# Queries of the expert stage: the first column group as two of 256, copies of x one order step later, a tile's end bank by bank

## The reference

```python
def block(hb):                                      # 128 tokens
    q = (hb @ w_query).reshape(128, 8, 2, 128)      # w_query: 2048 x 2048
    s = einsum('thpc,hpnc->thpn', q, sub_keys)      # two scores per head, 128 keys each
    top_s, top_i = lax.top_k(s, 16)
    cand_s = top_s[:, :, 0, :, None] + top_s[:, :, 1, None, :]
    cand_i = top_i[:, :, 0, :, None] * 128 + top_i[:, :, 1, None, :]
    best_s, best_j = lax.top_k(cand_s, 16)
    idx = take_along_axis(cand_i, best_j)           # 16 of 16384 experts
    g = softmax(best_s)
    a = gelu(einsum('thkd,td->thk', u[idx], hb))
    return einsum('thk,thkd->td', g * a, v[idx])    # added to x
```

## Time and profile before

| | |
|---|---|
| Runs, median (lowest, highest) | 3162.84 us (3162.42, 3167.22), three runs |
| The profiled execution's own time | 3161.82 us |
| Its span, from first to last instruction | 3159.6 us |
| Busy in the span | PE 69%, DVE 54%, ACT 27%, POOL 26% |
| Moved by DMA | 901 MB, 285 GB/s over the span |

### The profile page before, as it was taken

How to read it: one execution, slowest core, us unless ns; L and a number is a source line. 1 busy time by engine, 2 the same in 40 slices (tenths; PEclk the granted TensorE clock), 3 DMA queues, 4 the chain that set the end, 5 groups by cost and what they waited for, 6 DMA issues and landing times.

```text
span 3159.6 us, 30717 instructions
## 1 busy us (share of the span) xinstructions
PE 2164.9 (69%) x12338; PEld 1487.2 (47%) x12338; DVE 1692.1 (54%) x2583; ACT 853.3 (27%) x1267; POOL 806.4 (26%) x680
## 2 busy tenths in 40 slices
PE   5899999989999999999989973223222222322335
PEld 2666677877778787667668872000000000000001
DVE  3436556654756664343335688665565555565430
ACT  1333443443444454454545421000000000000000
POOL 1111100000000000000000026665555555555552
PEclk8999999999999999999989987665666666666667
DMA  9888865557665555343325689999999999999998
GB/s 385 285 294 271 287 213 153 181 166 243 207 190 157 152 178 158 116 134 106 107 86 162 207 323 406 422 422 421 422 421 422 421 422 420 422 421 422 421 422 338
DMA packets 243593, 901.00 MB, mean 285 GB/s; under 512 B 20374, under 2 KB 45228, under 8 KB 177004
## 3 DMA queue, kind: packets, MB, share of 16 engines
q0 software_dynamic: 94208, 612.85, 48.3%
q1 hardware_dynamic: 148768, 285.58, 27.9%
q10 hardware_dynamic: 476, 0.62, 0.1%
HBM read 894.78 MB, written 2.10 MB: 284 GB/s over the span
## 4 chain that ended last, share of the span: by engine, by line
PE 56%; DMA 30%; DVE 7%; ACT 3%; issue 2%; POOL 2%; SPq 0%; DVEq 0%; ACTq 0%; POOLq 0%
PE pp L1786 48%; DMA late<-in_peer_v,MI 9%; PE tp L1786 6%; DMA P<-in_peer_v,MI 5%; DMA x<-in_peer_v,MI 5%; DMA ring<-in_peer_v,MI 4%; DMA SY<-in_peer_v,MI 2%; DVE wL L1112 2%; PE tp L1789 2%; DMA late<-in_w_mod 2%; ACT wH L613 1%; DMA ring<-in_peer_w_query 1%; POOL late L2319 1%; DMA ring<-in_w_in 1%; DMA P<-in_w_mod 0%
## 5 line engine op out<-in xcount | busy, mean ns | idle before, releaser
L1112 DVE TENSOR_TENSOR wL<-ring,wH 128x1024 fp32r<-128x1024 f32 (+3 forms) x504 | 583.8, 1162 | 765.0 <-ACT wH L613 763.7
L1786 PE MATMUL pp<-wH,hH 128*128 128x512 f32 (+3 forms) x1888 | 747.8, 396 | 16.2 <-issue 7.9
L613 ACT ACTIVATE wH<-ring 128x1024 fp32r<-128x1024 f32 (+3 forms) x504 | 508.0, 1010 | 784.8 <-PE pp L1786 650.8
L1786 PE MATMUL pp<-wH,hL 128*128 128x512 f32 (+3 forms) x1888 | 718.3, 380 | 0.0
L1786 PE MATMUL pp<-wL,hH 128*128 128x512 f32 (+3 forms) x1888 | 717.7, 380 | 0.0
L1786 PE MATMUL pp<-late,S 128*32 128x512 f32 x768 | 234.5, 892 | 336.9 <-DMA x<-in_peer_v,MI 157.9
L1786 PEld LDWEIGHTS pp<-wH,hH 128*128 128x128 f32 x1888 | 360.0, 191 | 159.5 <-issue 90.6
L1786 PEld LDWEIGHTS pp<-wH,hL 128*128 128x128 f32 x1888 | 359.2, 190 | 63.6
L1786 PEld LDWEIGHTS pp<-wL,hH 128*128 128x128 f32 x1888 | 360.8, 191 | 56.1 <-issue 1.0
L1745 DVE CUSTOM_DVE_ANT_0 late<-late,P 128x2048 f32<-128x2048 f32 x84 | 191.3, 2288 | 154.0 <-DMA late<-in_peer_u,MI 153.8
L1786 PE MATMUL pp<-P,S 128*32 128x512 f32 x360 | 157.8, 873 | 166.8 <-DMA late<-in_peer_v,MI 91.4
(11 more groups left out here) (303 smaller groups left out, 2925.5 us busy)
## 6 DMA issues: line engine op xcount, KB each, us to landing
ring<-in_w_in SPq DMA_DIRECT2D x288, 512.0 KB, 4.0
ring<-in_w_out SPq DMA_DIRECT2D x96, 512.0 KB, 4.4
P<-in_w_mod POOLq DMA_DIRECT2D x85, 512.0 KB, 4.9
late<-in_w_mod SPq DMA_DIRECT2D x64, 512.0 KB, 9.4
SY<-in_w_mod POOLq DMA_DIRECT2D x43, 512.0 KB, 5.1
ring<-in_w_in SPq DMA_DIRECT2D x48, 368.0 KB, 4.6
ring<-in_peer_w_query SPq DMA_DIRECT2D x32, 512.0 KB, 7.2
ring<-in_w_in SPq DMA_DIRECT2D x24, 344.0 KB, 3.2
```

What stands on the lines that cost most here:

```text
L613: act(heads(wH[k % NB][:, 0:2 * wd], 2), raw, ACT.Copy).then_inc(*tick("act_hi", ("hi", k)))
L1112: tt(lo, raw, hi.bitcast(F32), ALU.subtract).then_inc(*tick("dve_lo", *names))
L1786: return e.matmul(o, l, r, start=start, stop=stop, skip_group_check=skip)
```

## The change

- `G_QUERY` makes the first group of `w_query` two groups of 256 columns, head 0 and head 1. There are now five groups and 40 pieces: 16 of 256 KB and 24 of 512 KB.
- The scores and the choice of head 0 are placed behind piece 8, those of head 1 behind piece 16. `FIRST_DOT` is 13, so that 27 dots stand between the pieces where there were 20.
- `hidden 0` and `hidden 1` move to pieces 8 and 10 (from 6 and 4). `nf` moves from `U` to `S`, since the scores of head 0 may now be written before hidden rows are read.
- The copies of x become a step of their own, `turn_x`, placed at piece 6, and `late_loads` moves into the projection before.
- At a tile's end each bank has its own mark `summed`, and is added as soon as it is complete. The stores are by bank, 32 rows x 512 columns of 64 KB each: 16 for a tile, 8 on SP's queue and 8 on ACT's.

```diff
-GROUPS = [G_IN, G_OUT, G_IN, G_OUT, G_IN2, G_OUT, G_OUT]
+G_QUERY = cgroups((0, 2, 256), (512, 3, 512))
+GROUPS = [G_IN, G_OUT, G_IN, G_OUT, G_IN2, G_OUT, G_QUERY]
...
-FIRST_DOT = 12
+FIRST_DOT = 13
...
         if n == 1:
             yield "sub_keys",
+            yield "late_loads",
...
-    yield "late_loads",
     for q, (g, c0, w, pc) in enumerate(PIECES[6]):
         yield from splits(6, q)
         if q == 3:
             yield "norm", 6
+        if q == 6:
+            yield "turn_x",
         if q == 2:
             yield "chunk", 6, 3
             yield "skip_pair",
-        if q in (4, 6):
-            yield "hidden", (6 - q) // 2
+        if q in (8, 10):
+            yield "hidden", q // 2 - 4
         yield "piece6", q
-        if g == 1 and pc == 0:
-            yield "scores", 0
+        if q in (8, 16):
+            yield "scores", 0, q // 16
             yield "skip_pair",
+        if q == 8:
             yield "open", "X", "choose", 0
-        if g == 1:
-            yield from pump(4, 0, 0)
-        if q == FIRST_DOT - 1:
+        if q in (8, 9):
+            yield from pump(3, 0, 0)
+        if 16 <= q < 23:
+            yield from pump(1, 0, 0)
+        if q == 23:
             yield "drain", "X"
         if q >= FIRST_DOT:
             yield "dot", 0, q - FIRST_DOT
...
-        nf = U[:, 0:2048]
+        nf = S[:, 0:2048]
...
-                if n == 34 - FIRST_DOT:
+                if n == len(PIECES[6]) + 2 - FIRST_DOT:
                     queue = list(range(5, NG)) + queue
...
+            def store_rows(t, parts, sem):
+                for d in range(4):
+                    w.wait_ge(*at("added", t, d))
+                    for q in parts:
+                        e.dma_start(rows_d[t, 32 * q:32 * q + 32, d * 512:(d + 1) * 512],
+                                    xP[q:128:4, t, d * 512:(d + 1) * 512]).then_inc(*landed(sem, ("out", t, d, q)))
...
-                    w.wait_ge(*at("added", t, 3))
-                    for q in range(4):
-                        e.dma_start(rows_d[t, 32 * q:32 * q + 32, :], P[q:128:4, 0, t * D:(t + 1) * D]).then_inc(
-                            *landed("out_done", ("out", t, q)))
+                    store_rows(t, (0, 1), "out_done")
...
-                    w.wait_ge(*at("mixed", 4 * t + 3, 7))
                     for d in range(4):
+                        w.wait_ge(*at("summed", t, d))
                         v = xP[:, t, d * 512:(d + 1) * 512]
                         tt(v, v, pp[d][:, :], ALU.add).then_inc(*tick("dve_h", ("added", t, d)))
...
+                elif what == "turn_x":
                     w.wait_ge(*at("x added", 5, 3, 1))
                     for t in range(2):
                         for q in range(4):
```

More of the change, by code:

```diff
@@ L345, in order @@
         if i < 7:
-            yield "scores", i + 1
+            yield "scores", i + 1, None
             yield "open", "X", "choose", i + 1
-        for j in range(0 if i else 32 - FIRST_DOT, 32):
+        for j in range(0 if i else len(PIECES[6]) - FIRST_DOT, 32):
             yield "dot", i, j
@@ L1066, in scalar @@
                     w.wait_ge(*at("turned", u))
-                    w.wait_ge(*(at("chosen", i - 2) if i > 1 else at("hidden", 0)))
-                    act(sc[i % 2], tp[u % 2][:, 0:512], ACT.Copy, scale=rsd[:, 4 + i // 4:5 + i // 4]).then_inc(*tick("act_h", ("pair free", u), ("scores", i)))
+                    if i > 1:
+                        w.wait_ge(*at("chosen", i - 2))
+                    w.wait_ge(*at("rstd", 6))
+                    h0, h1 = (0, 2) if a[1] is None else (a[1], a[1] + 1)
+                    act(sc[i % 2][:, 256 * h0:256 * h1], tp[u % 2][:, 0:256 * (h1 - h0)], ACT.Copy,
+                        scale=rsd[:, 4 + i // 4:5 + i // 4]).then_inc(
+                        *tick("act_h", ("pair free", u), *[("scores", i, h) for h in range(h0, h1)]))
+                elif what == "add":
+                    store_rows(a[0], (2, 3), "out_act_done")
                 elif what == "gelu":
@@ L2249, in tensor @@
                     w.wait_ge(*at("chunk", 6, pc // 2))
-                    for b in range(4):
+                    for b in range(wd // 128):
                         for k2 in range(2):
```

32 lines of the change are left out of this document (22 added, 10 removed).

## The result

| | kernel before | changed kernel |
|---|---|---|
| Median of 12 runs | 3164.22 us (3155.29 to 3171.22) | 3169.41 us (3161.94 to 3173.62) |
| Ratio, 95% interval | | 1.0019 [1.0011, 1.0027] |
| Span of the profiled execution | 3159.6 us | 3160.0 us |

The changed kernel is slower by 0.19%, some 6 us, and the interval lies clear of no change. The prediction had 3165.5 within 3156 to 3172, and 0.65 for a change under 0.2%; 3169.4 lies just above the 3169.2 that it named as that bound, the ratio just under it.

The account below looks back on a forecast made before the run. The prediction took DMA to bound the expert stage. Its terms, -5.1 + 10.4 + 0 - 2.5 = +2.8 us, gave 3164.6 for the profiled execution and 3165.5 for the median, range 3156 to 3172.

Parts of the forecast that it names:

- second rival: Expert stage, pieces 16 to 23: DVE becomes the bound with head 1's choice there; 7 us idle DMA, 3172.5, chance 0.17.
- first gather: Start of the expert stage: head 0 projected sooner, so the first gather comes 5.1 us earlier, bounds 13 and 3.4.
- left to move behind it: Loads behind the first gather: 24 of 512 KB instead of 16, 4.19 MB more, costing 10.4 us at 401 GB/s.
- gaps behind the first gather: Mixed stretch of gathers and loads: no added DMA idle time, 0 us, bounds -2.7 and +5.
- end of a tile: Last adds and stores: three of four adds fall under the matmuls, saving 2.5 us, bounds 1.9 and 3.2.
- The copies of x: Query projection: copies issued where they stood, starving loads beside them; PE idles 5.9 us ahead of piece 6, then half clock.
- The rival that rested on it: Query projection: loads don't starve beside the copies, first gather 13 us earlier, total 3157.7, chance 0.17.
- DVE stays behind cover: From head 0's numbers to the last cut: DVE needs 96.7 us, DMA 107, so DVE adds no time.
- The sign of the last paragraph: Mixed stretch: the forecast is wrong if the DMA share falls under 0.95.
- The other sign: Start of the expert stage: the forecast is wrong if the first gather comes before 1825.
- The gaps close: Third rival: 2.7 us lost behind the first gather and 2.6 around the last cut vanish; 3160.3, chance 0.06.
- The second choice of POOL's: Unit 1's choice, after the last cut: POOL's 6.96 us wait grows by up to 2 under queued transfers, costing 0.

Follow-up runs that it names:

- e4: Changed kernel with head 1's choice in one block behind piece 16 instead of a step behind each of pieces 16 to 22; ratio 1.0019 to the kernel before.
- e6: Changed kernel without head 1's choice for unit 0, its expert numbers copied from head 0; ratio 1.0011 to the kernel before.
- e2: Changed kernel with the copies of x made to wait for the cut of piece 6; ratio 1.0003 to the kernel before.
- e3: Changed kernel with the copies of x made to wait for the cut of piece 10; ratio 1.0005 to the kernel before.
- e5: Changed kernel with the 16 loads of pieces 24 to 39 bringing only 128 of their 256 rows; ratio 1.0004 to the kernel before.
- e7: Changed kernel with copies of x behind the cut of piece 6 and both hidden instructions behind head 0's numbers; ratio 1.0004 to the kernel before.
- e1: Kernel before with only the new end of a tile put in; ratio 0.9993 to the kernel before.
- e8: Changed kernel with copies and hidden instructions later, cuts between head 0's choice steps, head 1's choice ahead of the first dot; ratio 1.0002 to the kernel before.
- e9: As e8, but each of the eight copies of x waits for a cut of its own, pieces 6 to 13; ratio 0.9988 to the kernel before.

## Why the prediction was right or wrong

**The range held, one term of the sum didn't, and part of the hit is luck.** The forecast's sum was +2.8 us; the pair of profiles has +7.2 and the runs some +6. By its own mechanism the forecast spanned 3161 to 3169, which 3169.4 just misses; the range held it because it reached nearly to the second rival's price. In the sum a first gather that came earlier than forecast hid a third of the term that failed. The terms, as the prediction put them, and as measured:

| Term | forecast | measured |
|---|---|---|
| first gather | -5.1 (-13 to -3.4) | -7.4 |
| left to move behind it | +10.4 | +10.0 |
| gaps behind the first gather | 0 (-2.7 to +5) | +6.8 |
| end of a tile | -2.5 (-3.2 to -1.9) | -2.3 |
| sum | +2.8 | +7.2 |

**The copies of x:** right. They were issued 1.2 us behind the first query matmul (before 1.3), and a load beside them took 12.0 us. PE stood 4.3 us instead of 5.9, in two pauses instead of one (in e4 and e6, the same up to there, in one of 4.3), and head 0 was projected at 18.7 us instead of 20.8 behind the first query matmul: the 1.6 us less of idle time are most of that. The half clock came as forecast: 0.50 over the 12 matmuls of piece 6, which took 2.9 us, and full pace again in piece 7. From there to the first gather it was 16.1 us, 16.3 forecast. The rule of the Trainium skill that queues take turns packet by packet ("DMA: Bandwidth & Descriptors", Queues, rings and completion order) was read as giving the loads a fair part. It speaks of packets, and says that such a packet holds some 9 to 17 descriptors; whether the profile's packets are these, no run here shows. Counted in the profile's packets one stretch looks like it (97 to 112, with 5.5 KB against 1 KB still only 15% of the time); the stretches with 63 to 27, 89 to 226, and 59 to none don't agree. The rival that rested on it failed, but its first gather, 13 us earlier, is what e2 and e3 have (42.2 - 29.3 = 12.9), once the copies wait.

**The bytes:** right, 24 loads and 4.22 MB. e5 adds what the term hid: such bytes are worth their transfer time only while DMA decides. Taking as many out again was worth 5.7 us.

**The gaps: the step that failed.** "DVE stays behind cover" came from a sum over the whole stretch, 96.7 us of DVE work in 107 us of DMA work. The sum was good (from head 0's numbers to the last cut, 112 us, DVE worked 94.8); the mean was the wrong question. A piece with a step of the choice needs up to 5.7 us of DVE where DMA needs 3.74, the others have only a tenth to spare, and what is in flight (five sets) didn't carry the difference beyond 1863. The prediction had this as its second rival, at 0.17, with a price of 7 us; e6 measured 6.9, for some 10 us less of DVE work (11.7 in e4's block, of which e6 keeps 1.5), and e7 showed that other DVE work behind the first gather is charged too. The sign of the last paragraph came: a share of 0.93 from 1870 to 1900, under its 0.95, and 0.82 from 1863 to 1886. So did the condition that the rival named: DVE waited for the starved loads of four cuts (0.8 to 2.2 us each, the last until 1858.8), and from then on every set had landed before its dot began. The other sign, a first gather before 1825, came only in time from the span's start (1821.0): counted from the first query matmul, its bound is 32.0 and the gather came at 34.8. The rival should have had the better part of the chance, since its working (4.8 us of DVE for a piece against 3.9 of DMA) needed no guess, and the one thing against it, the absorbing by what is in flight, was only asserted. With that rival's 3172.5 and the 2.3 us by which the first gather was forecast too late, the time would have come out at 3170.2; the median was 3169.4.

**The gaps close** (the third rival): mostly not. The first 10 us behind the first gather lost 3.6 us (3.0 before), the 9.8 us at the last cut 1.5 (2.6 before, in 11.5).

**The second choice of POOL's** (unit 1): forecast to wait up to 2 us longer than the 6.96 of the earlier trace rows, and to cost nothing. It waited 7.29:

```profile
1972.20 0.94 POOL L2349 DMA_INDIRECT late<-in_peer_u,MI  x1 [7.29 <-DVE MI L1691]
```

**The end:** right, mechanism and size (the profiles of after and e1; the ratio of e1 alone doesn't tell it from nothing).

## What to carry to other kernels

When one resource decides and a second runs at 90% of it, a forecast has to be made piece by piece and not for the stretch: work that a change puts on the second, in the time when it refills the first, is charged for the most part (here 6.9 us for some 10, and 3.8 for 2.35). In the kernel before the same choice stood under the first five gathers, and 6.9 us less were lost; but e8, which put it back there with more beside it, lost 4.5 us more than the kernel before, so the place alone doesn't make it free. Halving a first unit of work to reach the next stage sooner also halves what is moved under its wait; the bytes left for later are a term of the sum, here larger than the gain. And a step that is moved in the order has moved only if the queue that issues it shows another instruction or another wait ahead of it.

## What the runs showed of the hardware

- Loads beside a block of copies from another queue got from 0 to 31% of the DMA engines in stretches of 2 us, in the first 10 us of the copies. The one in the chain took 12 us to land with 256 KB as with 512 KB: both times it landed 0.4 us behind the last copy, so halving it did not shorten its wait. With half the columns its packets were 1 KB instead of 1.9, against the copies' 5.5; whether that matters, no run shows. Copies that go one at a time, each with a load (e9), or behind the loads that matter (e2), leave PE with one pause of 0.4 us ahead of head 0's end.
- Loads that land late need not cost anything: with DMA at a share of 1.01 to 1.03 four of them took 17.2 us each (median) and nothing was lost; DMA lost 7 us in the 23 us behind that, where loads took 8.1.
- The first half, in which these kernels compute the same, differs by up to 9.5 us between profiled executions (first query matmul 1786.25 to 1795.75), with the granted clock at 0.88 and 0.83 in one and 1.00 and 0.91 in another for the same 80 us. A difference of 0.2% between two kernels is read much better from a mark inside the program than from the time of the whole.
